# Fourth and fifth product of the down stage exchanged, and 512-column shared-weight terms in two products of each gate/up pair

## The reference

```python
x = x + rms_norm(mixed, g_post_mix)
h2 = rms_norm(x, g_pre_ffn)
ff = (jax.nn.silu(h2 @ w_gate) * (h2 @ w_up)) @ w_down
return x + rms_norm(ff, g_post_ffn)
```

## Time and profile before

| | us |
|---|---|
| median of 3 runs | 586.13 (585.72 to 586.18) |
| the profiled execution | 585.19 |
| its span, first to last instruction | 583.5 |
| PE busy | 573.6 (98%) |
| DVE busy | 459.5 (79%) |
| ACT busy | 314.6 (54%) |
| POOL busy | 127.5 (22%) |
| mean granted TensorE clock | 0.998 |

### The profile page before, as it was taken

How to read it: one execution, slowest core, us unless ns; L and a number is a source line. 1 busy time by engine, 2 the same in 40 slices (tenths; PEclk the granted TensorE clock), 3 DMA queues, 4 the chain that set the end, 5 groups by cost and what they waited for, 6 DMA issues and landing times.

```text
span 583.5 us, 9854 instructions
## 1 busy us (share of the span) xinstructions
PE 573.6 (98%) x3517; PEld 511.9 (88%) x3517; DVE 459.5 (79%) x740; ACT 314.6 (54%) x520; POOL 127.5 (22%) x136
## 2 busy tenths in 40 slices
PE   7999999999999999999999999999999999999996
PEld 5878888888888878899999999999999998888884
DVE  4768888888768864779888887978798678888787
ACT  7636666566544544547353544445363465547752
POOL 1111011132200010063423223242423004344100
PEclk9999999999999999999999999999999999999999
DMA  7643433334123470302232313232231449999833
GB/s 296 179 151 111 120 94 108 125 92 127 55 74 120 137 285 36 109 37 72 77 141 77 140 72 144 72 110 106 102 113 72 144 151 286 261 215 205 163 144 144
DMA packets 27322, 76.82 MB, mean 132 GB/s; under 512 B 3194, under 2 KB 3194, under 8 KB 27292
## 3 DMA queue, kind: packets, MB, share of 16 engines
q1 hardware_dynamic: 18204, 54.83, 26.8%
q0 software_dynamic: 9088, 21.61, 16.9%
HBM read 69.06 MB, written 4.22 MB: 126 GB/s over the span
## 4 chain that ended last, share of the span: by engine, by line
PE 96%; DMA 1%; DVE 1%; ACT 1%; issue 0%; SPq 0%; DVEq 0%; ACTq 0%
PE bank L1765 12%; PE bank L1764 12%; PE bank L1763 12%; PE bank L1511 11%; PE bank L1513 11%; PE bank L1512 11%; PE bank L1817 6%; PE bank L1821 6%; PE bank L1819 6%; PE bank L1645 3%; PE bank L1633 2%; PE bank L1557 2%; PE bank L1623 1%; PE bank L1621 1%; DMA x_sb<-in_x 1%; PE bank L1604 1%
## 5 line engine op out<-in xcount | busy, mean ns | idle before, releaser
L1765 PE MATMUL bank<-tok_hi,form_lo 128*128 128x256 f32 x320 | 90.6, 283 | 0.0
L1764 PE MATMUL bank<-tok_lo,form_hi 128*128 128x256 f32 x320 | 90.6, 283 | 0.0
L1763 PE MATMUL bank<-tok_hi,form_hi 128*128 128x256 f32 x320 | 90.6, 283 | 0.0
L1511 PE MATMUL bank<-hn_hi,w_hi 128*128 128x512 f32 (+2 forms) x200 | 78.8, 394 | 0.1
L1513 PE MATMUL bank<-hn_hi,w_lo 128*128 128x512 f32 (+2 forms) x200 | 77.0, 385 | 0.0
L1512 PE MATMUL bank<-hn_lo,w_hi 128*128 128x512 f32 (+2 forms) x200 | 76.8, 384 | 0.0
L1765 PE MATMUL bank<-hn_hi,form_lo 128*128 128x256 f32 x240 | 67.9, 283 | 0.0
L1764 PE MATMUL bank<-hn_lo,form_hi 128*128 128x256 f32 x240 | 67.9, 283 | 0.0
L1763 PE MATMUL bank<-hn_hi,form_hi 128*128 128x256 f32 x240 | 67.9, 283 | 0.0
L1763 PEld LDWEIGHTS bank<-tok_hi,form_hi 128*128 128x128 f32 x320 | 61.4, 192 | 0.0
L1764 PEld LDWEIGHTS bank<-tok_lo,form_hi 128*128 128x128 f32 x320 | 61.4, 192 | 0.0
(11 more groups left out here) (199 smaller groups left out, 1394.2 us busy)
## 6 DMA issues: line engine op xcount, KB each, us to landing
raw<-in_w_in_units SPq DMA_DIRECT2D x24, 512.0 KB, 3.4
raw<-in_w_gate_units SPq DMA_DIRECT2D x22, 512.0 KB, 3.3
raw<-in_w_up_units SPq DMA_DIRECT2D x22, 512.0 KB, 4.2
down_x<-in_w_down POOLq DMA_DIRECT2D x15, 512.0 KB, 11.6
down_y<-in_w_down SPq DMA_DIRECT2D x10, 512.0 KB, 11.6
raw<-in_w_out SPq DMA_DIRECT2D x8, 512.0 KB, 3.3
q_lh<-q_hl POOLq DMA_DIRECT2D x12, 256.0 KB, 2.8
down_x<-in_w_down SPq DMA_DIRECT2D x5, 512.0 KB, 4.3
```

The source lines that it names most:

```text
L1511: nc.tensor.matmul(out_ap, sh, mh, start=first, stop=False)
L1763: nc.tensor.matmul(out_ap, sh, mh, start=first and k == 0, stop=False, skip_group_check=True)
L1764: nc.tensor.matmul(out_ap, sh, ml, start=False, stop=False, skip_group_check=True)
L1765: mm = nc.tensor.matmul(out_ap, sl, mh, start=False, stop=k == HK - 1, skip_group_check=True)
```

## The change

Gate/up pairs: hn_hi and hn_lo become two halves of one tile hn_hl. For P1 and P2, `wide_product` sends for each k the high weight part against [hi, lo] tokens, 512 columns, into the whole bank (hi x hi in the lower half, hi x lo in the upper), and the low weight part against the hi tokens, 256 columns, into the lower half. The sum of the halves is made outside PE: ACT copies the upper half to SBUF, and DVE adds the lower half to it, once after P1 (`sum_p1`, for which V6 and PE's P2 wait) and once after P2 (`sum_c11`, for which SiLU waits).

Down stage: the products that were fourth and fifth change places, the first of the two in a bank pair of its own (D), the other in A. The order of its DMAs (weights of products 3 and 4) changes with it. The sum with a12 is made in place of a12, while PE works on product 2, together with the sum before it. `join_c12` takes the place of a copy and a join; `join_u2` subtracts the state of A after product 4, for which product 4 ends and product 5 begins tile by tile. The table load for Sqrt is placed in product 1.

```diff
-DOWN_CHAIN = ((A_BANK, True), (B_BANK, True), (C_BANK, True), (A_BANK, False), (C_BANK, False), (A_BANK, False),
+DOWN_CHAIN = ((A_BANK, True), (B_BANK, True), (C_BANK, True), (D_BANK, True), (A_BANK, False), (A_BANK, False),
...
+DOWN_SUMS_BEFORE = {2: 2, 3: 6, 5: 8}
...
-                add_down("x", 1, 0, 3, g)
+                add_down("y", 0, 1, 3, g)
             for g in range(DG):
-                add_down("y", 0, 1, 4, g)
+                add_down("x", 1, 0, 4, g)
...
-                if 2 <= n <= 5:
-                    act_e.wait_ge(down_sum, 2 * (n - 1))
+                if n in DOWN_SUMS_BEFORE:
+                    act_e.wait_ge(down_sum, DOWN_SUMS_BEFORE[n])
...
-                nc.scalar.copy(sp_s1[:, :], bank[:, SBANKS[par][0], 0:HALF]).then_inc(s1_done, 1)
+                nc.scalar.copy(sp_s1[:, :], bank[:, SBANKS[par][0], HALF:SEQ]).then_inc(s1_done, 1)
...
                 act_e.wait_ge(prod, q * 7 + (P2 + 1))
...
+                nc.scalar.copy(sp_c11[:, :], bank[:, SBANKS[par][0], HALF:SEQ]).then_inc(c11_kept, 1)
+                act_e.wait_ge(c11_done, q + 1)
                 act_e.wait_ge(act_done, q + 1)
-                nc.scalar.activation(silu_g[:, par, 0:HALF], bank[:, SBANKS[par][0], 0:HALF], ACT.Silu
-                                     ).then_inc(silu_done, 1)
+                nc.scalar.activation(silu_g[:, par, 0:HALF], sp_c11[:, :], ACT.Silu).then_inc(silu_done, 1)
...
             for s in range(2, 4 * DG):
+                if s == DG + 1:
+                    nc.scalar.preload_act_table(ACT.Sqrt)
                 down_hi(s)
                 if s % DG == 3:
                     down_form_hi(s // DG + 1)
...
+            def sum_p1(q, par):
+
+                dve.wait_ge(s1_done, q + 1)
+                nc.vector.tensor_tensor(sp_s1[:, :], bank[:, SBANKS[par][0], 0:HALF], sp_s1[:, :], ALU.add
+                                        ).then_inc(p1_done, 1)
+
+            def sum_c11(q, par):
+
+                dve.wait_ge(c11_kept, q + 1)
+                nc.vector.tensor_tensor(sp_c11[:, :], bank[:, SBANKS[par][0], 0:HALF], sp_c11[:, :], ALU.add
+                                        ).then_inc(c11_done, 1)
...
+                if m == 0:
+                    dve.wait_ge(act_done, FT)
+                else:
+                    dve.wait_ge(down_sum, 2 * m)
+                if m in (1, 3):
+                    dve.wait_ge(da_lo_done, 2 * (m + 2))
+                dst, in0, in1, op = ((down_s, a21, a22, ALU.subtract), (down_s, down_s, a11, ALU.subtract),
+                                     (a12, down_s, a12, ALU.add), (down_s, a11, a21, ALU.subtract))[m]
+                nc.vector.tensor_tensor(dst[:, k, :], in0[:, k, :], in1[:, k, :], op).then_inc(down_sum, 1)
...
+            def join_u2():
+
+                dve.wait_ge(joined, 2)
+                for t in range(2):
+                    if t == 0:
+                        dve.wait_ge(u2_done, 1)
+                    else:
+                        dve.wait_ge(dw_used, DG * 5)
+                    nc.vector.tensor_tensor(c12[:, t, :], c12[:, t, :], bank[:, A_BANK + t, :], ALU.subtract
+                                            ).then_inc(joined, 1)
...
+                sum_p1(q, par)
                 sum_v6(q, par)
...
+                sum_c11(q, par)
                 up_first(q, par)
...
                 down_lo(s)
-                if g in (1, 2) and 2 <= n + 1 <= 5:
-                    down_sums(n + 1, g - 1)
+                if g in (1, 2) and n in (1, 2, 4):
+                    down_sums({1: 0, 2: 1, 4: 3}[n], g - 1)
+                if g in (2, 3) and n == 2:
+                    down_sums(2, g - 2)
...
+            def wide_product(bank_no, par, form, mv, first):
+
+                for k in range(HK):
+                    mh, m_hl = mv(k)
+                    nc.tensor.matmul(bank[:, bank_no, :].rearrange("p (two n) -> p two n", two=2),
+                                     form_hi[par][:, form, k, :], m_hl, start=first and k == 0, stop=False,
+                                     skip_group_check=True)
+                    mm = nc.tensor.matmul(bank[:, bank_no, 0:HALF], form_lo[par][:, form, k, :], mh, start=False,
+                                          stop=k == HK - 1, skip_group_check=True)
+                mm.then_inc(prod, 1)
...
-                pe.wait_ge(s1_done, q + 1)
-                block_product(a_bank, par, A12, direct(HK, 0), False)
+                pe.wait_ge(p1_done, q + 1)
+                wide_product(a_bank, par, A12, direct_wide(HK, 0), False)
...
+            pe.wait_ge(da_lo_done, 2 * 5)
+            pe.wait_ge(kept, 1)
+            groups_in_turn(4, range(DG - 2))
+            groups_by_tile(4, tail, None, u2_done)
+            pe.wait_ge(da_lo_done, 2 * 6)
+            groups_by_tile(5, first, 3, None)
+            groups_in_turn(5, middle)
+            groups_by_tile(5, tail, None, u3_done)
```

More of the change, by code:

```diff
@@ L396, in hybrid_block @@
         s1_done = sem("s1_done")
+        p1_done = sem("p1_done")
+        c11_kept = sem("c11_kept")
+        c11_done = sem("c11_done")
         post = sem("post")
@@ L424, in down_form @@
             if n == 1:
+                return act[:, DK:FT, first]
+            if n == 3:
                 return act[:, DK:FT, first]
@@ L1401, in join, with join_c12 @@
                 last.then_inc(joined, 1)
+            def join_c12():
+                dve.wait_ge(dw_used, DG * 4)
+                dve.wait_ge(kept, 2)
+                for t in range(2):
+                    last = nc.vector.tensor_tensor(c12[:, t, :], bank[:, D_BANK + t, :], c22[:, t, :], ALU.add)
+                last.then_inc(joined, 1)
+            def join_u2():
+                dve.wait_ge(joined, 2)
+                for t in range(2):
+                    if t == 0:
[4 more added lines that the diff above has]
+                                            ).then_inc(joined, 1)
             second_sum(0, 0)
@@ L1463, in _ @@
                         join(1, c11, True, ALU.add, 1)
-                    if n == 5:
-                        join(4, c12, True, ALU.subtract, 3)
+                    if n == 4:
+                        join_c12()
+                if s == 5 * DG + 1:
+                    join_u2()
             for t in range(2):
@@ L1830, in down_group, with groups_in_turn, groups_by_tile @@
                 return mm
[L1832 removed]
+            pe.wait_ge(c11_done, LAST_Q)
             pe.wait_ge(post, 5 * LAST_Q)
[L1834 removed]
+            def groups_in_turn(n, groups):
+                for g in groups:
+                    pe.wait_ge(dw_lo_done, DG * n + g + 1)
+                    down_group(n, g, range(2)).then_inc(dw_used, 1)
+            def groups_by_tile(n, groups, before, after):
+                for t in range(2):
+                    if before is not None:
+                        pe.wait_ge(joined, before + t)
+                    for g in groups:
+                        if t == 0:
+                            pe.wait_ge(dw_lo_done, DG * n + g + 1)
+                        mm = down_group(n, g, (t,))
+                        if t == 1:
+                            mm.then_inc(dw_used, 1)
+                    if t == 0 and after is not None:
+                        mm.then_inc(after, 1)
+            first, middle, tail = range(TAIL_GROUP), range(TAIL_GROUP, DG - 2), range(DG - 2, DG)
+            for n in range(4):
                 pe.wait_ge(da_lo_done, 2 * (n + 1))
                 if n == 1:
[L1837 removed]
+                    pe.wait_ge(c11_done, SP_PAIRS)
                     pe.wait_ge(post, 5 * SP_PAIRS)
[L1839 to L1850 removed]
+                groups_in_turn(n, range(DG))
+            pe.wait_ge(da_lo_done, 2 * 5)
[6 more added lines that the diff above has]
+            groups_by_tile(5, tail, None, u3_done)
             pe.wait_ge(da_lo_done, 2 * DOWN_PRODUCTS)
```

52 lines of the change are left out of this document (19 added, 33 removed).

## The result

The changed kernel takes 589.47 us (median of 6 runs, 588.54 to 590.69), the kernel before in the same batch 586.15 (6 runs, 585.61 to 586.56): ratio 1.006, 95% interval 1.0047 to 1.0073. It is slower by 3.3 us, between 2.8 and 4.3. The forecast was 588.5, 1.0 us too low, inside the range of 586.3 to 590.8.

A forecast was written before the change was run, and what follows sets the result against it. TensorE (PE) matmul issue was taken as the bound, 96% of the chain. Terms -2.1 + 3.98 + 0.36 + 0.16 = +2.4 gave 587.6 us for the profiled execution, 588.5 for the median; range 586.3 to 590.8.

The forecast's parts named there:

- The relay (+3.98): Down stage around product 3: third sum delays ACT's form and weight splits by 4.34 us; PE loses 3.98 us.
- Product 5 (+0.36): Before product 5 in the down stage: DVE's subtraction ends at 15.2, PE wants it at 14.96; 0.4 us lost with signalling.
- The restarts (+0.16): After PE's gaps in the down stage: slower first starts, two binding gaps, 0.16 us.
- The merges (-2.1): Gate/up pairs, P1 and P2: 160 merges into 512-column matmuls save 13.1 ns each, 2.1 us.
- Pair 0 (0 to 0.1): First gate/up pair, DVE backed up, tightest slack: the added adds cost 0 to 0.1 us once.
- rival D: Pairs' thin slacks break, or PE's clock falls to 1.2 GHz after the gap: some 2 us more, 590.5; chance 0.08.
- The DMA waits of ACT in product 3 go; they are not on PE's path: Down stage: exchanged DMAs each due two products after issue, so these waits vanish; counted at nothing.
- Rival A: Down stage: the sums fit into slack, PE loses 0 to 0.5 us; 584.3; chance 0.10.
- B: Pairs: merging wins nothing, two runs costing as two matmuls or fixed time in the column stream; 590.6; chance 0.11.
- C: Down stage: DVE and ACT get ahead early, some 2 of the 4.34 us absorbed; 586.5; chance 0.09.

The follow-up runs named there:

- e7: Changed kernel plus 64 already satisfied waits ahead of PE's first matmul; 589.64 us, ratio 1.0062.
- e2: Changed kernel's down-stage exchange alone, with the gate/up pairs of the kernel before; 590.17 us, ratio 1.007.
- e4: Changed kernel without the third sum (addition to a12 left out, product 3 takes a12 as it is); 584.85 us, ratio 0.998.
- e9: Changed kernel reordered: form 3 behind three weight splits on ACT and DVE, product 5's last sum one group earlier; 585.55 us, ratio 0.9985.
- e5: Changed kernel with P2's 512-column matmuls reading one run of hn_hi instead of two of 256; computation altered; 589.73 us, ratio 1.0068.
- e1: New gate/up pairs alone, with the down stage of the kernel before; 586.12 us, ratio 1.0004.
- e10: e9 with the four 512-column matmuls of a shared product first, then its four of 256; 584.94 us, ratio 0.9982.
- e8: Kernel before plus 192 already satisfied waits ahead of PE's first matmul; 592.42 us in a single run.

## Why the prediction was right, and where not

- **The relay (+3.98): right in place, mechanism and size.** 4.34 was the path through the third sum, 4.36 is measured; 0.39 was what the pairs' two adds cost ACT, and ACT's first split of the down stage starts 474.73 - 472.83 = 1.90 after PE's first matmul, before 1.52: 0.38. The three gaps were forecast as 2.0, 0.8 and 1.2; where no late load reached PE they are 1.97, 0.61 and 1.13 (e7), 3.71 together. e2 shows it alone, e4 takes its cause away, e9 its order.
- **Product 5 (+0.36): right.** 0.35, with its restart 0.43.
- **The restarts (+0.16): too small.** Four places instead of two pay about 0.1: 0.37. The prediction counted two binding gaps, and named three and a fourth before product 5 itself.
- **The merges (-2.1): the step that was mis-sized.** They gave 1.27. The distance of 0.227 was read from a stretch of equal 512-column matmuls and used for a 512 between 256s, where it is 0.235. The bounds held (nothing to 2.1), and the value was taken at their good end. The Trainium skill, page "TensorE: Matmul & The Clock Gate", section "Back-to-back issue gap", would have given 2.5 ns for a merge and 0.4 us in all; measured are 8 ns alternating and 11 grouped, so trace and rule both missed, on either side.
- **Late loads (nothing predicted): +0.67 in the profiled execution,** not there in e5 and e7. This term was not seen at all; no row of before hinted at it.
- **Pair 0 (0 to 0.1): right.** One matmul starts 0.07 late at 279.83, and no other wait of PE shows in the pairs; the slacks of rival D held. PE's granted clock stayed at the upper level, 2.4 GHz, over the 2.5 us gap: it is 1.00 in the stretch from 516.3 to 519.8, and behind the restart at 516.32 the starts come 0.23 to 0.24 apart (516.65, 516.89, 517.12).
- **"The DMA waits of ACT in product 3 go; they are not on PE's path": half right.** They go. But they were on the path's edge: e1 shows that without the exchange they eat the pairs' gain whole. The two parts of the change are not independent. The exchange may buy something once its own relay is cured: e9 is 0.9 us better than e1 by the stages of one execution each, and 0.6 by the medians, but there the two intervals overlap, so this is not shown.

The sum again with measured sizes: -1.27 for the pairs, +4.56 for a down stage with no late load, together +3.29; the medians say +3.3. The forecast of +2.4 lacked 0.8 at the merges; the down stage as a whole was forecast at +4.50 and missed by 0.06, since gaps 0.27 shorter and restarts 0.2 larger nearly cancel. Rival A (hidden relay) is refuted by the gaps; B, as "nothing won", by the stretch of 200.32, though two fifths of the gain did go the way it pointed; C by the gaps, of which 3.71 of the forecast 3.98 us arrived; D by the clock and the slacks.

**Open.** Why a 512 beside a 256 is followed 7 ns later than a 512 beside a 512, and why 2 ns remain when they are grouped: one run or two is not it (e5). What makes SP's issues long: the fetch of instructions falls on the long one of the first three in every kernel with new pairs, no experiment moved it at will, and it doesn't cover the long seventh and eighth. Why a long issue reaches PE in one execution (after, e4, e9) and not in another (e5, e7, e10). How e1's loss divides between PE's earlier arrival and the later additions. And e4's gap in its short executions.

## What to carry to other kernels

When a step puts more work ahead of an in-order wait, count what is queued behind that wait and does not need it: here four weight splits stood behind one form, and putting three of them in front, with one sum a group earlier, gave back 4.2 of 5.2 us without removing any work. A stage whose waits all hide can still have little slack: before crediting a gain upstream, ask what the next stage's transfers are paced by, and how much earlier they would be wanted. And take a duration from a row whose neighbours are like those of the place where it will stand.

## What the runs showed of the hardware

- The distance after a 512-column matmul depends on what follows: 0.227 us in a row of 512s of the down stage, 0.2325 in groups of four, 0.235 when 256s alternate with them; the 256 behind it then takes 0.117 instead of 0.120.
- Moving operands of two runs of 256 columns, 16 KB apart, stream as fast as one run of 512 (0.236 both in P2, e7 against e5).
- Accumulating DMAs of 512 KB on POOL's queue landed one every 2.5 us during product 3, in the kernel before and in e1 alike. Earlier, while SP's loads landed between them, it was one every 4.0 to 4.1 us (490.30, 494.32, 498.43 and 502.42 in the kernel before). They set the pace of a stage that wants them sooner.
- Among SP's first three issues of loads for the down stage, one took 1.25 to 1.68 us instead of 0.43 to 0.47 in ten kernels, always the one on which an instruction fetch of 16 KB fell, the second in nine and the third in e5; no fetch and no long issue among the first three in before, e2 and e8.
- After a wait of PE in the down stage, of 0.2 to 2.5 us, the first two starts lie 0.31 to 0.34 us apart instead of 0.227, and the granted clock stays at 1.00.
- A tile of x at the start of the kernel landed up to 1.9 us late, in some executions of the same program head and not in others. Single profiled executions that differ by a microsecond are best compared stage by stage.
